# Full-causal value slabs first and with tokens on the partitions; VectorE takes five low parts of weights

## The reference

```
h = rms_norm(x, g_mix)
qa,ka,va,qb,kb,vb,gate_a,gate_b = split(h @ w_in)    # 512,512,512,512,128,128,1024,1024 wide
ya = causal attention, 8 heads of 64 (qa, ka rms-normed per head, relative-position bias)
yb = window-128 attention, 8 q heads on 2 kv heads, per-head sinks, same norms and bias
x  = x + w_out( sigmoid(gate_a) * (ya @ w_branch_a) + sigmoid(gate_b) * (yb @ w_branch_b) )
x  = x + W2 relu(W1 rms_norm(x))^2                   # 1024 -> 4096 -> 1024
```

## Time and profile before

| | |
|---|---|
| median of 3 runs | 678.23 us (677.71 to 678.46) |
| the profiled execution | 677.42 us |
| its span | 675.6 us |
| PE busy | 671.0 us (99%), 3254 matmul records |
| DVE, ACT, POOL busy | 500.7, 369.6, 322.4 us |
| granted TensorE clock | 9 tenths or more in all 40 slices |
| matmul lines L1335 to L1337 | 65% of the chain that ended last |

### The profile page before, as it was taken

The page is one execution under the profiler, slowest core; times in us unless marked ns, Lnnn a source line. Parts: engine busy times, 40 slices in busy tenths (PEclk is TensorE's granted clock), DMA queues, the critical chain, the costliest instruction groups (busy, mean ns, idle before and its releaser), DMA issues.

```text
span 675.6 us, 9503 instructions
## 1 busy us (share of the span) xinstructions
PE 671.0 (99%) x3254; PEld 555.3 (82%) x3254; DVE 500.7 (74%) x697; ACT 369.6 (55%) x662; POOL 322.4 (48%) x194
## 2 busy tenths in 40 slices
PE   9999999999999999999999999999999999999998
PEld 7888788888888888888888888888888888888886
DVE  7875898455555555885558879788797888978897
ACT  7765676666665666543348546254463525536360
POOL 0175566455556553444436436246362454435532
PEclk9999999999999999999999999999999999999999
DMA  8223242222322213555222231414133151230303
GB/s 320 94 88 100 69 122 94 80 69 89 108 89 73 69 53 110 156 175 192 85 95 93 96 119 65 155 62 151 66 102 115 62 186 62 93 98 27 125 0 125
DMA packets 22909, 69.87 MB, mean 103 GB/s; under 512 B 2731, under 2 KB 4267, under 8 KB 22876
## 3 DMA queue, kind: packets, MB, share of 16 engines
q1 hardware_dynamic: 22588, 68.92, 30.5%
q10 hardware_dynamic: 288, 0.52, 0.2%
HBM read 67.27 MB, written 2.16 MB: 103 GB/s over the span
## 4 chain that ended last, share of the span: by engine, by line
PE 97%; ACT 1%; DMA 1%; POOL 0%; issue 0%; DVE 0%; SPq 0%
PE bank L1335 22%; PE bank L1337 22%; PE bank L1336 21%; PE bank L1645 8%; PE bank L1644 8%; PE bank L1642 8%; PE bank L1482 2%; PE bank L1495 2%; PE bank L1515 1%; PE bank L1517 1%; DMA store<-x_t 1%; PE bank L1614 1%; PE bank L1361 0%; PE bank L1362 0%; PE bank L1423 0%; POOL w_lo L505 0%
## 5 line engine op out<-in xcount | busy, mean ns | idle before, releaser
L505 POOL TENSOR_TENSOR w_lo<-w_raw,w_hi 128x1024 fp32r<-128x1024 f32 x77 | 190.6, 2480 | 229.1 <-ACT w_hi L594 229.0
L1335 PE MATMUL bank<-x_hi,w_hi 128*128 128x512 f32 x326 | 131.3, 403 | 0.5 <-DVE store L1078 0.4
L1337 PE MATMUL bank<-x_hi,w_lo 128*128 128x512 f32 x326 | 127.5, 391 | 0.0
L1336 PE MATMUL bank<-x_lo,w_hi 128*128 128x512 f32 x326 | 127.0, 390 | 0.0
L1335 PE MATMUL bank<-qk_hi,w_hi 128*128 128x512 f32 x320 | 125.0, 391 | 0.0
L1337 PE MATMUL bank<-qk_hi,w_lo 128*128 128x512 f32 x320 | 124.6, 389 | 0.0
L1336 PE MATMUL bank<-qk_lo,w_hi 128*128 128x512 f32 x320 | 124.5, 389 | 0.0
L594 ACT ACTIVATE w_hi<-w_raw 128x1024 fp32r<-128x1024 f32 x80 | 83.8, 1056 | 57.2 <-PE bank L1337 57.2
L1218 DVE SCALAR_TENSOR_TENSOR store<-bank,softmax,store 128x512 f32<-128x512 f32 x101 | 71.9, 742 | 23.8 <-PE bank L1645 23.8
L1645 PE MATMUL bank<-v_parts,x_lo 128*128 128x512 f32 (+1 forms) x218 | 84.4, 387 | 0.0
L1642 PE MATMUL bank<-v_parts,x_hi 128*128 128x512 f32 (+1 forms) x218 | 84.4, 387 | 0.0
(11 more groups left out here) (167 smaller groups left out, 1177.6 us busy)
## 6 DMA issues: line engine op xcount, KB each, us to landing
w_raw<-slabs SPq DMA_DIRECT2D x80, 512.0 KB, 3.3
bias_m<-slabs SPq DMA_DIRECT2D x16, 512.0 KB, 3.5
qk_hi_again<-slabs SPq DMA_DIRECT2D x16, 512.0 KB, 5.0
store<-x_t SPq DMA_DIRECT2D x16, 256.0 KB, 3.8
bias_m<-tab_dram SPq DMA_DIRECT2D x8, 256.0 KB, 4.2
out<-store SPq DMA_DIRECT2D x7, 256.0 KB, 2.1
bias_m<-tab_dram SPq DMA_DIRECT2D x8, 128.0 KB, 3.6
w_raw<-slabs ACTq DMA_DIRECT2D x1, 384.0 KB, 4.0
```

The lines of the kernel that those rows point to most:

```text
L505: pool.tensor_tensor(w_lo[:, g % WS, :], w_raw[:, g % RAW, :], w_hi[:, g % WS, :].bitcast(F32), ALU.subtract).then_inc(w_lo_ready, 1)
L1335: pe.matmul(out_, wh, xh, start=first, stop=False)
L1336: pe.matmul(out_, wh, xl, start=False, stop=False)
L1337: last = pe.matmul(out_, wl, xh, start=False, stop=end)
```

## The change

The four v slabs of attention "a" come first, as slabs 0 to 3, in another layout: slab j holds the rows of k tiles 2j and 2j + 1 for all 512 value channels. In their products x is the stationary side (128 tokens of it) and the weights move: `va_product`, for each k tile 4 token tiles x 3 matmuls of 128x512, into four banks at once. The result has tokens on the partitions. These slabs need no transposes; ACT (`va_hi`) and DVE (`va_lo`) scale and split them from the banks. The scale is now per partition, so four float32 matmuls with one column (`mean_squares`) give the mean square per token, with a small root chain.

The pieces of the first two slabs become halves (FIRST = 4), and slab 1 is loaded after four tiles of x. Then come k, four q, k and q four times (slabs 4 to 16), and the one v slab of "b" as slab 17. Queries are written reversed and not keys and values. SCORE_GROUPS starts with steps 0 and 1.

DVE_LOWS gives w_lo of slabs 8, 10, 12, 14 and 16 to DVE.

```diff
RAW, WS = 4, 2
-FIRST = 2
+FIRST = 4
 WARM_UP = 10
-QKV_KIND = ["k", "q", "q", "v", "q", "v", "q", "v"] + ["k", "q"] * 4 + ["v"] * 2
-QKV_TILE = [0, 1, 2, 0, 3, 1, 4, 2] + [5, 9, 6, 10, 7, 11, 8, 12] + [3, 4]
-FIRST_A = 8
+N_VA = 4
+QKV_KIND = ["va"] * N_VA + ["k", "q", "q", "q", "q"] + ["k", "q"] * 4 + ["v"]
+QKV_TILE = [None] * N_VA + [0, 1, 2, 3, 4] + [5, 9, 6, 10, 7, 11, 8, 12] + [0]
+FIRST_A = 9
 Y_B, Y_A = 1, 9
...
-        v_parts = sb("v_parts", [P, 5, QT, 4, HD], R)
+        v_parts = sb("v_parts", [P, 5, D], R)
+        vb_parts = v_parts[:, 0, :].rearrange("p (r a d) -> p r a d", r=QT, a=4)
+        va_parts = v_parts[:, 1:5, :].rearrange("p j n -> p (j n)").rearrange(
+            "p (r t a d) -> p r t a d", r=QT, t=4, a=4)
...
+        LAST_Q, LAST_V = N_QKV - 2, N_QKV - 1
+        DVE_LOWS = (8, 10, 12, 14, 16)
+        def ss_bank(n):
+            return bank[3 + n % 2] if n < N_QK - 1 else acc(LAST_Q - 2)
         def key_tiles(i, qt):
-            return QT - 1 - qt, min(2, qt + 1) if i < 8 else qt + 1
+            nk = min(2, qt + 1) if i < 8 else qt + 1
+            return qt + 1 - nk, nk
...
-        SCORE_GROUPS = [(0, 1, 2), (3, 4, 5), (6, 7, 8), (9, 10, 11), (12, 13), (14, 15)]
+        SCORE_GROUPS = [(0, 1), (2, 3, 4), (5, 6, 7), (8, 9, 10), (11, 12, 13), (14, 15)]
...
+                if k == 4:
+                    load_first(sp, 1)
+                    load_rest(sp, 1)
                 sp.dma_start(store[:, k, :], x_t[k]).then_inc(x_arrived[k], 16)
-            load_first(sp, 1)
-            load_rest(sp, 1)
...
             for s in range(4, G_GATE + 2):
-                split_lo(s, s + 3)
-                for g in {5: (0, 1), 6: (2,)}.get(s, (s - 4,) if s > 6 else ()):
-                    if not is_v(g):
-                        qk_split_lo(g)
+                if s - 1 in DVE_LOWS:
+                    pool.wait_ge(w_lo_ready, s - 1)
+                if s not in DVE_LOWS:
+                    split_lo(s, s + 3)
+                if s - 4 >= N_VA:
+                    qk_split_lo(s - 4)
+                if step == 2:
+                    qk_split_lo(LAST_Q)
...
+                if k == 4:
+                    act.wait_ge(w_hi_ready, 2)
+                    hi_part(1, slice(0, FIRST * P), first_arrived[1])
+                    hi_part(1, slice(FIRST * P, D), arrived[1])
+            split_hi(2)
...
+            def va_hi(r):
+                act.wait_ge(slab_done, N_VA)
+                act.wait_ge(r_col_ready, 2)
+                act.activation(va_hi_part[r], va_tile(r), ACT.Copy,
+                               scale=r_col[:, r:r + 1]).then_inc(va_hi_ready, 1)
             split_hi(3)
-            qkv_square(0)
-            qkv_square(1)
+            split_hi(4)
+            act.wait_ge(ms_ready, 1)
+            power(c_root, c_root_sq, c_inv_sq, c_root_ready, 3)
+            act.wait_ge(ms_ready, 2)
+            power(r_root, r_root_sq, r_inv_sq, r_root_ready, 3)
+            split_hi(5)
+            for r in range(QT):
+                va_hi(r)
...
-            for g in range(2, N_QKV):
+            for g in range(N_VA, N_QKV):
                 split_hi(g + 2)
                 if g == 7:
                     table_hi()
                 if not is_v(g):
                     qkv_square(g)
...
-                if g >= 4 and not is_v(g - 2):
+                if g - 2 >= N_VA:
                     qkv_hi(g - 2)
-                if is_v(g - 1):
-                    v_hi(g - 1)
-                if g > 3 and not is_v(g - 1):
+                if g - 1 >= N_VA:
                     qkv_root(g - 1)
...
+                if k == 4:
+                    split_first(1)
+                    split_rest(1)
+            split_lo(2, 2)
...
-            def x_mean_square():
+            def x_mean_squares():
                 dve.wait_ge(ms_done, 1)
+                dve.tensor_scalar(c_inv_sq, bank[4][:, 0:QT], EPS, None, ALU.add).then_inc(ms_ready, 1)
+                dve.wait_ge(ms_done, 2)
                 dve.tensor_scalar(r_inv_sq, bank[5][:, :], EPS, None, ALU.add).then_inc(ms_ready, 1)
-                dve.wait_ge(ms_ready, 1)
+                dve.wait_ge(c_root_ready, 3)
+                refine(r_col, c_root, c_root_sq, c_inv_sq, r_col_ready, 2)
+                dve.wait_ge(r_root_ready, 3)
+                refine(r_all[:, :], r_root, r_root_sq, r_inv_sq, r_ready, 2)
+            def va_lo(r):
+                dve.wait_ge(va_hi_ready, r + 1)
+                dve.scalar_tensor_tensor(out=va_lo_part[r], in0=va_tile(r), scalar=r_col[:, r:r + 1],
+                                         in1=va_hi_part[r].bitcast(F32), op0=ALU.mult,
+                                         op1=ALU.subtract).then_inc(va_lo_ready, 1)
...
-            qk_split_squares(0)
-            qk_split_squares(1)
-            x_mean_square()
-            qk_mean(0)
-            qk_mean(1)
-            for g in range(2, N_QKV):
+            x_mean_squares()
+            for r in range(QT):
+                va_lo(r)
...
                     qk_split_squares(g)
                 else:
                     v_scale(g)
...
-                if is_v(g - 1):
-                    v_split_lo(g - 1)
-                if g > 3 and not is_v(g - 1):
+                if g + 2 in DVE_LOWS:
+                    dve.wait_ge(w_lo_ready, g + 1)
+                    split_lo(g + 2, 1)
+                if N_VA <= g - 1 < LAST_Q:
                     qk_norm(g - 1)
                 if not is_v(g):
...
-                        v_split_lo(N_QKV - 1)
+                        v_split_lo(LAST_V)
+                        qk_norm(LAST_Q)
...
-            def mean_square(out_):
+            def mean_squares(column, out_):
+                pe.wait_ge(xsum_ready, KT - 1)
+                for r in range(QT):
+                    last = pe.matmul(column[:, r:r + 1], x_sum[:, P * r:P * r + P], ones[:, :],
+                                     start=True, stop=True)
+                last.then_inc(ms_done, 1)
                 mean = mean_ones.to_broadcast([P, P])
                 pe.wait_ge(xsum_hi_ready, 1)
...
-            AFTER = {(3, 0): 0, (3, 2): 1, (3, 7): 2, (5, 3): 3}
-            AFTER.update({(g, KT - 1): g - 1 for g in range(5, N_QKV)})
...
+            def va_weight(kt):
+                g, at = kt // 2, slice(S * (kt % 2), S * (kt % 2) + S)
+                return w_hi[:, g % WS, at], w_lo[:, g % WS, at]
+            def va_product(kt, r, n):
+                high, low = va_weight(kt)
+                if n == 0:
+                    pe.wait_ge(x_hi_ready, kt + 1)
+                elif n == 1:
+                    if kt % 2 == 0 and kt < 4:
+                        pe.wait_ge(first_ready, kt // 2 + 1)
+                    elif kt < 4:
+                        pe.wait_ge(rest_ready, kt // 2 + 1)
+                else:
+                    pe.wait_ge(x_lo_ready, kt + 1)
+                part, moving = ((x_hi, high), (x_hi, low), (x_lo, high))[n]
+                return pe.matmul(acc(r)[:, :], keys_part(part, kt, r), moving, start=(kt == 0 and n == 0),
+                                 stop=(kt == KT - 1 and n == 2))
             for kt in range(KT):
+                if kt < 4:
+                    pe.wait_ge(w_hi_ready, kt + 1)
                 else:
+                    pe.wait_ge(w_lo_ready, kt // 2)
+                if kt < 2:
+                    order = [(r, n) for n in range(3) for r in range(QT)]
+                else:
+                    order = [(r, n) for r in range(QT) for n in range(3)]
+                for r, n in order:
+                    last = va_product(kt, r, n)
+                if kt % 2:
+                    last.then_inc(slab_done, 1)
+                if kt == 5:
+                    mean_squares(bank[4], bank[5])
+            AFTER = {(g, KT - 1): g - 1 for g in range(N_VA + 1, LAST_V)}
+            AFTER[LAST_V, 4] = LAST_Q
+            for g in range(N_VA, N_QKV):
+                pe.wait_ge(w_lo_ready, g)
                 if g >= 5:
                     qkv_read(g - 5)
                 for kt in range(KT):
                     last = slab_part(g, acc(g), from_x, [kt], kt == 0, kt == KT - 1)
                     if (g, kt) in AFTER:
                         after(AFTER[g, kt])
                     if (g, kt) in ((10, 2), (11, 2)):
                         table_product(g - 10)
...
             pe.wait_ge(qk_lo_ready, qk_count(FIRST_A))
-            pe.wait_ge(ss_read, N_QK)
-            qkv_read(N_QKV - 2)
+            pe.wait_ge(ss_read, N_QK - 1)
             for step in range(STEPS):
                 if step == 2:
                     pe.wait_ge(pre_ready, N_QK)
                     pe.wait_ge(pre_v_ready, N_V)
                     pe.wait_ge(v_lo_ready, N_V)
...
-    qb, va = qb.reshape(D, 4, P), va.reshape(D, 4, P)
-    w_qkv = np.concatenate([kb, qb[:, 0], qb[:, 1], vb, qb[:, 2], va[:, 0], qb[:, 3], va[:, 1], *kq,
-                            va[:, 2], va[:, 3], ga, gb], axis=1)
```

(15 more changed lines are left out.)

138 lines of the change are left out of this document (48 added, 90 removed).

## The result

The changed kernel takes **679.54 us** (median of 14 runs, 677.7 to 680.34), the kernel before 678.22 in the same session (14 runs, 677.62 to 678.87): ratio of the runs 1.0015 with a 95% interval of 1.0008 to 1.0022 (the two medians alone give 1.0019). The profiled execution took 679.53 us, its span is 677.7 (677.42 and 675.6 before). A median of 679.8 was predicted.

What follows compares the result with a forecast made beforehand. PE's own stream and its new waits were taken as the bound: -1.76 + 0.88 - 0.3 + 0.64 + 2.7 - 0.6 = +1.56 us, so 677.42 becomes 679.0 profiled, 679.8 median, against 678.23. Range for 8 in 10: 676.6 to 682.2.

Steps and rivals of the forecast that it cites:

- transposes: Value slabs: 16 transposes in four groups leave PE's stream, 0.44 us a group, -1.76 us.
- columns: Four added one-column float32 matmuls for the mean square per token, two records each at 0.11 us: +0.88 us.
- front: First microseconds: each x tile feeds 12 matmuls, not 3, so starvation from 7.20 to 8.65 us goes: -0.3 us.
- wait (a): Inside slab 17: slab 16's norm sums wait for DVE's low part of the square, slowed beside POOL: +0.64 us.
- wait (b): End of stage: scores of steps 2 to 4 wait for DVE's maxima, behind the norm of slab 16: +2.7 us.
- wait for gate scaling: PE's old wait for DVE's scaling of the first gate slab goes: -0.60 us.
- part 3: VectorE takes five low parts of weights at 1.22 us each; hidden beside PE's slab, so it costs nothing.
- third rival: VectorE's low parts arrive late, stopping PE 0.5 to 1 us in each of five slabs: 682.3 to 684.8 us; chance 0.1.
- part 2: First microseconds: first matmul stays at 5.89 us, less starvation afterwards, no wait for the sum over x squared: -0.3 us.
- 1.6 us of slack, no wait: Front: DVE has the sum over x squared at 21.5 us, PE wants it at 23.1 us.
- part 4: End of stage, slab 16 right before slab 17: two new waits, +0.64 and +2.7 us, and -0.60 us for gate scaling.
- second rival: Both end waits shorter, the one in slab 17 gone, the later 1.8 us, columns 0.44: 677.8 us; chance 0.22.

Runs made afterwards that it cites:

- slab 18 run: Kernel with slab 16's norm ahead of v's low part on DVE (677.14 us), plus slab 18's low part of weights moved to DVE: 676.26 us, ratio 0.9975.
- the order on DVE: The changed kernel with the norm of slab 16 put ahead of the low part of v on DVE at step 0: 677.14 us, ratio 0.9986.
- slab 18 alone: Kernel with slab 16's norm ahead, v's low part behind step 1's maxima and six DVE_LOWS slabs (675.64 us), cut to slab 18 only: 675.56 us, ratio 0.9965.
- run with PE kept busy: The changed kernel with ten unread 128x512 matmuls on PE ahead of the wait before the scores of step 2: 677.95 us, ratio 0.9999.

## Why the prediction was right, and where it was not

By the prediction's own steps, first profile of the change (679.53 us) and second (677.86):

| step | predicted | first | second |
|---|---|---|---|
| transposes | -1.76 | -1.76, by 0.44 a group | same |
| columns | +0.88 | +0.82 | +0.80 |
| front | -0.3 | -0.2 | -0.4 |
| wait (a) | +0.64 | +0.56 | +0.56 |
| wait (b) | +2.7 | +2.38 | +2.37 |
| wait for gate scaling | -0.60 | -0.60 | -0.60 |
| gap at 148 us, in the kernel before alone | not seen | -0.25 | -0.25 |
| clock behind (b) | not seen | +1.54 | 0 |
| sum | +1.56 | +2.5 | +0.7 |
| profiled execution | +1.56 | +2.11 | +0.44 |

The "front" figures compare the start of the same later matmul (the 96th of 512 columns: 28.57 us before, 29.18 and 28.95 after) less the columns. The columns' figures are start to start, to the matmul behind them. The gap at 148 us follows a group of transposes: the kernel before takes 0.71 us from 147.68 to 148.39 us where 0.44 to 0.46 is usual. 0.3 to 0.4 us of each sum is not accounted for: the executions are that much shorter than the steps add up to.

The table sets profile against profile, and the kernel before was profiled in an execution 0.8 us under its own median; those of the change lie within 0.2 us of the middle of their groups. The prediction added those 0.8 us to the change as well (679.0 to 679.8), and that term did not come. Median against median the upper group is 1.4 to 1.5 us slower than the kernel before and the lower one 0 to 0.3 faster, in each case 0.7 to 1.1 us less than the steps add up to.

**Right.** The bound was PE's own stream, and what counted was what PE does and waits for. Both new waits came where they were put, for the reasons given. For (a) the slab 18 run shows it; the sum was 0.64 against 0.56. For (b) the order on DVE shows it. One-column float32 matmuls leave two records each, 0.10 us apiece. Value matmuls keep the spacing of 0.227 us.

**Mis-sized.** The term for a moved low part in part 3, "+ 1.22": for the five in the stage the median is 2.33 us, since each but one stands behind POOL's qk_lo, which starts with it:

```profile
97.68 0.69 DVE L997 TENSOR_TENSOR pt_lo<-store,pt_hi 128x512 fp32r<-128x512 f32 x1
98.29 2.33 DVE L968 TENSOR_TENSOR w_lo<-w_raw,w_hi 128x1024 fp32r<-128x1024 f32 x1
100.54 0.68 DVE L985 SCALAR_TENSOR_TENSOR store<-store 128x512 f32<-128x512 f32 x1
...
98.24 1.29 POOL L542 TENSOR_TENSOR qk_lo<-store,qk_hi 128x512 fp32r<-128x512 f32 x1 [3.21 <-ACT qk_hi L679]
```

The square's low part of 0.7 us in the even slabs (L997) came as forecast. The mechanism of the third rival is there (qk_lo holds the moved low part), but not its condition, a delay of 1 us more: the low part ends at 100.62 us and no matmul of slabs 6 to 16 starts late. The Trainium skill, page "SBUF — State Buffer", section "Who interferes with whom", says that a DVE instruction with two SBUF inputs and a GpSimd one that reads SBUF contend, and that the order of issue decides who is held. L968, L988 and L983 above agree: 2.33, 1.67 and 2.85 us beside POOL against 1.22, 0.69 and 0.69 alone.

**Wrong.** Two steps. In part 2, "1.6 us of slack, no wait" rested on DVE having the sum over x squared at 21.5 us. In the new order it has it at 23.05 us (22.36 + 0.69), 0.2 us ahead of PE, and in the profiles of the runs with slab 18 on DVE and with slab 18 alone PE waits 0.23 us for a part of this sum. And the step left out what is queued behind the sum, DVE's low part of slab 3:

```profile
22.36 0.69 DVE L981 TENSOR_TENSOR pt_hi<-store,pt_hi 128x512 fp32r<-128x512 f32 x1
22.41 0.95 PE L1445 MATMUL bank<-ones,store 128*128 128x1 f32 x8
...
22.97 1.22 DVE L968 TENSOR_TENSOR w_lo<-w_raw,w_hi 128x1024 fp32r<-128x1024 f32 x1
...
23.55 0.40 PE L1452 MATMUL bank<-pt_hi,pt_lo 128*128 128x512 f32 x1
...
24.25 0.50 PE L1482 MATMUL bank<-w_hi,x_hi 128*128 128x512 f32 x1 [0.30 <-DVE w_lo L968]
```

It ends at 24.19 us and PE wanted it at 23.78. The wait is 0.47 us here and absent in the second profile, where slab 2 had arrived 0.2 us earlier and PE came 0.4 later. That the front still gains 0.2 us has another reason, which the prediction had set aside: "slow however they are fed" did not hold. The first two groups of four matmuls, first profile and then second:

```profile
6.01 1.15 PE L1482 MATMUL bank<-w_hi,x_hi 128*128 128x512 f32 x4 [0.98 <-ACT x_hi L648]
7.00 1.07 PE L1482 MATMUL bank<-w_lo,x_hi 128*128 128x512 f32 x4
```

```profile
5.83 1.72 PE L1482 MATMUL bank<-w_hi,x_hi 128*128 128x512 f32 x4 [0.27 <-ACT x_hi L648]
7.39 1.09 PE L1482 MATMUL bank<-w_lo,x_hi 128*128 128x512 f32 x4
```

The first four take 0.99 us from start to start in the first profile and 1.56 in the second (0.99 to 1.56 over the profiles of all kernels with this front). So ahead of the columns the 72nd matmul of 512 columns starts 0.89 us earlier than in the kernel before in the first profile (22.19 against 23.08 us) and 0.46 in the second (22.62), where 0.3 was taken. The other 0.6 of the first profile differs from execution to execution of the same kernel, and why is open; it goes into the wait of 0.47 and a slower restart.

In part 4, the term of 2.7 us for wait (b) counted an idle PE at its length. It costs more: 17 of 25 runs of the change have the mean clock of 0.997 and lie some 1.5 to 1.8 us higher, and the one trace among them has the granted clock at the 1.2 GHz level behind the wait, 1.54 us on top. Leave that out and my sum is 1.1 us too high (1.56 against 0.44), not far from the price of the clock. The median was hit because a missing cost cancels several small excesses: 0.3 in (b), 0.25 at 148 us, 0.25 in (a), the columns and the front, and the 0.3 not accounted for. That is luck, and the 0.8 us from profile to median, which only the kernel before has, is part of it: 679.0 was predicted for the profiled execution, and it took 679.53. The runs without the fall, 677.9, lie where the second rival stood, though not by its mechanism: (a) was there and (b) was 2.37 and not 1.8. That it would come out slower rests on the clock; without it the change is no change (677.95 in the run with PE kept busy, ratio 0.9999).

## What to carry to other kernels

When a value's place in the order changes, follow what each engine has queued behind the moved work, on the front as much as at the end; the change took 0.9 us of work off TensorE, net, and lost it to one wait for a chain whose last three operations could have begun in a hole of 3 us on the same engine. Behind a new wait on TensorE of the length seen here, read the granted clock in a narrow stretch of the trace, and look at the spread of the runs: two groups with two mean clocks point to it, and matmuls that nobody reads, put into the gap, tell the wait's price from the clock's. Work moved from GpSimd to VectorE is priced by its duration beside GpSimd (2.33 us here), not alone (1.22).
